# Two of three matrix products of a feed-forward block regrouped after Strassen, on one NeuronCore

## The reference

```python
def swiglu(x, w_gate, w_up, w_down):
    return (jax.nn.silu(x @ w_gate) * (x @ w_up)) @ w_down
...
h = h + 0.5 * swiglu(rms_norm(h, ffn1_norm[l]), ffn1_w_gate[l], ffn1_w_up[l], ffn1_w_down[l])
...
h = h + 0.5 * swiglu(rms_norm(h, ffn2_norm[l]), ffn2_w_gate[l], ffn2_w_up[l], ffn2_w_down[l])
```

## Time and profile before

| | us |
|---|---|
| median of 3 runs | 1800.49 (1800.37 to 1800.58) |
| the profiled execution: first to last instruction | 1798.8 |
| PE busy | 1790.1 (100%) |
| DVE busy | 1072.4 (60%) |
| ACT busy | 775.2 (43%) |
| POOL busy | 206.1 (11%) |

### The profile page before, as it was taken

How to read it: one execution, slowest core, us unless ns; L and a number is a source line. 1 busy time by engine, 2 the same in 40 slices (tenths; PEclk the granted TensorE clock), 3 DMA queues, 4 the chain that set the end, 5 groups by cost and what they waited for, 6 DMA issues and landing times.

```text
span 1798.8 us, 22927 instructions
## 1 busy us (share of the span) xinstructions
PE 1790.1 (100%) x8322; PEld 1472.2 (82%) x8322; DVE 1072.4 (60%) x1339; ACT 775.2 (43%) x1103; POOL 206.1 (11%) x174
## 2 busy tenths in 40 slices
PE   9999999999999999999999999999999999999998
PEld 7888888888777788888888888888888888888887
DVE  6444443342778665444443348877577586868985
ACT  5333332223555544333333335454353454466673
POOL 3000000011000002000001110110201102213333
PEclk9999999999999999999999999999999999999999
DMA  4332333344321232332233323232222222233233
GB/s 157 99 99 93 94 105 105 105 145 131 110 77 60 70 95 94 97 101 93 93 99 106 107 93 105 89 99 94 83 94 87 93 85 80 85 106 106 94 129 117
DMA packets 51506, 178.63 MB, mean 99 GB/s; under 512 B 6168, under 2 KB 8344, under 8 KB 51440
## 3 DMA queue, kind: packets, MB, share of 16 engines
q1 hardware_dynamic: 48624, 169.10, 29.4%
q0 software_dynamic: 2384, 8.21, 1.5%
q10 hardware_dynamic: 432, 0.40, 0.1%
HBM read 173.48 MB, written 2.11 MB: 98 GB/s over the span
## 4 chain that ended last, share of the span: by engine, by line
PE 98%; DVE 1%; ACT 0%; DMA 0%; issue 0%; POOL 0%; ACTq 0%; DVEq 0%
PE banks L548 29%; PE banks L550 29%; PE banks L549 29%; PE banks L711 1%; PE banks L730 1%; PE banks L754 1%; PE banks L889 1%; PE banks L891 1%; PE banks L890 1%; PE banks L917 0%; PE banks L915 0%; PE banks L916 0%; PE banks L674 0%; PE banks L675 0%; PE banks L676 0%; PE banks L1101 0%
## 5 line engine op out<-in xcount | busy, mean ns | idle before, releaser
L1784 DVE TENSOR_TENSOR w_lo<-w_raw,w_hi 128x1024 fp32r<-128x1024 f32 x313 | 397.5, 1270 | 528.5 <-ACT w_hi L1187 527.6
L548 PE MATMUL banks<-u_hi,w_hi 128*128 128x512 f32 x1528 | 599.5, 392 | 0.8 <-DVE u_lo L1801 0.8
L550 PE MATMUL banks<-u_hi,w_lo 128*128 128x512 f32 x1528 | 595.0, 389 | 0.0
L549 PE MATMUL banks<-u_lo,w_hi 128*128 128x512 f32 x1528 | 594.6, 389 | 0.0
L1187 ACT ACTIVATE w_hi<-w_raw 128x1024 fp32r<-128x1024 f32 x313 | 331.4, 1059 | 512.5 <-PE banks L550 475.1
L548 PEld LDWEIGHTS banks<-u_hi,w_hi 128*128 128x128 f32 x1528 | 286.9, 188 | 61.6 <-issue 2.4
L550 PEld LDWEIGHTS banks<-u_hi,w_lo 128*128 128x128 f32 x1528 | 286.8, 188 | 60.5
L549 PEld LDWEIGHTS banks<-u_lo,w_hi 128*128 128x128 f32 x1528 | 287.0, 188 | 58.9 <-issue 0.5
L548 PE MATMUL banks<-hid_hi,w_hi 128*128 128x512 f32 x352 | 136.9, 389 | 0.0
L549 PE MATMUL banks<-hid_lo,w_hi 128*128 128x512 f32 x352 | 136.9, 389 | 0.0
L550 PE MATMUL banks<-hid_hi,w_lo 128*128 128x512 f32 x352 | 136.9, 389 | 0.0
(11 more groups left out here) (342 smaller groups left out, 2425.9 us busy)
## 6 DMA issues: line engine op xcount, KB each, us to landing
w_raw<-weights SPq DMA_DIRECT2D x315, 512.0 KB, 3.5
bias<-neighbour_bias POOLq DMA_DIRECT2D x8, 384.0 KB, 5.1
v_win<-v_a POOLq DMA_DIRECT2D x16, 128.0 KB, 5.0
out_t<-x SPq DMA_DIRECT2D x16, 128.0 KB, 1.8
x<-x_t SPq DMA_DIRECT2D x3, 512.0 KB, 6.7
nm<-gate_rows POOLq DMA_DIRECT2D x4, 256.0 KB, 4.1
fl<-gate_rows POOLq DMA_DIRECT2D x4, 256.0 KB, 3.6
rope<-rope_table POOLq DMA_DIRECT2D x1, 512.0 KB, 5.5
```

The lines of the kernel that those rows point to most:

```text
L548: nc.tensor.matmul(o, wh, hi, start=start and k == 0, stop=False)
L549: nc.tensor.matmul(o, wh, lo, start=False, stop=False)
L550: ins = nc.tensor.matmul(o, wl, hi, start=False, stop=stop and k == len(pairs) - 1)
L1784: nc.vector.tensor_tensor(w_lo[:, n.slot, :], w_raw[:, n.slot, :], w_hi[:, n.slot, :].bitcast(F32), ALU.subtract)\
```

## The change

Of the 22 chunks of gate and up, 6 stay as they were. The other 16 are taken in 8 pairs of two chunks. For a pair the weights are a 2 x 2 arrangement (up and gate; first and second half of the width), the values too (halves of the width; halves of the tokens). Their 8 partial products become 7, after Strassen's scheme in Winograd's form, with 256 tokens each. Product k of pair p is (k, p) in the list `SP_SEQ` (56 products, 24 matmuls with 256 columns each).

- **Values.** DVE writes the normalised values in full (`full`, to `uf`, 8 instructions beside the last plain chunks), makes four sums of quarters (`combo_sum`), and both engines split these and three plain quarters (`combo_high`, `quarter_high` on ACT; `combo_low`, `quarter_low` on DVE: 7 of each).
- **Weights.** POOL loads five matrices of 512 KB a pair (`load_matrices`): `m1` (two buffers), `m2`, `m3`, `m4` and `mx` (one buffer each). DVE makes four sums in place (`first_sums` two, `later_sum`, `last_sum`). Each of the seven is split by `mat_high` (ACT) and `mat_low` (DVE) into one of four buffers (`slot_of`), so product j reuses that of product j-4.
- **Results.** Products 1, 6, 7, 4 add up in one bank; ACT copies its state after 1, 6 and 7 (`snap_p1`, `snap_p6`, `snap_p7`) and takes silu of it after 4 (`silu_first`), and the next of them waits for the copy. DVE adds products 2, 5 and 3 to the copies (`up_first`, `gate_second`, `up_second`), then `silu_second` (ACT), `hid_first`, `hid_second` (DVE), `pair_high` (ACT), `pair_low` (DVE).
- **Down.** The 22 blocks of a column are summed in three parts, of chunks 0 to 5, 6 to 13 and 14 to 21. Each part has 8 columns, one unit each, each added to `x` by itself. The first stands after the plain chunks, the second after product (1, 5), the third after the last product.

TensorE's waits in `pair_product`, beside `m_lo` for the weights: product 1 waits for `silu_first` two pairs earlier; 6, 7 and 4 for the copy after 1, 6 and 7; 3 for `gate_second`; 2 and 5 for the sums two pairs earlier. `snap_p1` to `snap_p7` wait for their product.

```diff
+F_PLAIN = 6
+N_SP = 8
+DOWN_PARTS = (range(0, F_PLAIN), range(F_PLAIN, 14), range(14, F_CHUNKS))
+U_FFN = 2 * F_PLAIN + 3 * DC
...
+def sp_products():
+    seq = [(5, 0), (1, 0), (6, 0), (2, 0), (7, 0)]
+    for p in range(N_SP - 1):
+        seq += [(1, p + 1), (4, p), (5, p + 1), (6, p + 1), (3, p), (7, p + 1), (2, p + 1)]
+    return seq + [(4, N_SP - 1), (3, N_SP - 1)]
+SP_SEQ = sp_products()
+N_PROD = len(SP_SEQ)
+SP_AT = {kp: j for j, kp in enumerate(SP_SEQ)}
+SP_SLOT = [(j + 2) % 4 for j in range(N_PROD - 1)] + [2]
+SP_SLOT_FREE = [max([i for i in range(j) if SP_SLOT[i] == SP_SLOT[j]], default=None) for j in range(N_PROD)]
+SP_LAST_IN = [max(j for j in range(N_PROD) if SP_SLOT[j] == k) for k in range(2)]
+DOWN1_AFTER = SP_AT[1, 5]
+DOWN1_SLOT_FREE = [max(j for j in range(DOWN1_AFTER + 1) if SP_SLOT[j] == k) for k in range(2)]
+SP_BANKS = ((3, 4), (5, 6), (7, 2))
+H1, H2 = slice(0, T // 2), slice(T // 2, T)
...
+        def slot_of(pair, pair2, j):
+            k = SP_SLOT[j]
+            return pair[:, k, :] if k < 2 else pair2[:, k - 2, :]
+        def product_source(k, p):
+            return (None, m1[:, p % 2, :], m2[:, :], m2[:, :], m4[:, :], mx[:, :], m1[:, p % 2, :], m3[:, :])[k]
...
+            def pair_product(f, j):
+                k, p = SP_SEQ[j]
+                q = N_SP * f + p
+                o = bank[SP_BANKS[{2: 1, 5: 2, 3: 2}.get(k, 0)][p % 2]]
+                pe.wait_ge(m_lo, N_PROD * f + j + 1)
+                if j == 0:
...
+                wh, wl = slot_of(w_hi, w_hi2, j), slot_of(w_lo, w_lo2, j)
+                fresh = k in (1, 2, 5)
+                for c in range(2):
+                    for kk in range(4):
+                        if k <= 3:
+                            kh, half = QUARTERS[k - 1]
+                            hi, lo = u_hi[:, 4 * kh + kk, half], u_lo[:, 4 * kh + kk, half]
+                        else:
+                            t = (T4, T1, T2, T3)[k - 4]
+                            hi, lo = xs_hi[:, t, kk * 256:(kk + 1) * 256], xs_lo[:, t, kk * 256:(kk + 1) * 256]
+                        b = slice((2 * kk + c) * P, (2 * kk + c + 1) * P)
+                        half_bank = o[:, c * 256:(c + 1) * 256]
+                        nc.tensor.matmul(half_bank, wh[:, b], hi, start=fresh and c == 0 and kk == 0, stop=False, skip_group_check=True)
+                        nc.tensor.matmul(half_bank, wh[:, b], lo, start=False, stop=False, skip_group_check=True)
+                        ins = nc.tensor.matmul(half_bank, wl[:, b], hi, start=False, stop=kk == 3, skip_group_check=True)
+                ins.then_inc(m_used, 1)
...
+            def down_columns(f, part, u0, g0):
+                chunks = DOWN_PARTS[part]
+                for m in range(DC):
+                    n, g = Lin(u0 + 2 * F_PLAIN + DC * part + m), Lin(g0 + 2 * F_PLAIN + DC * part + m)
+                    unit_ready(n)
+                    bank_free(g)
+                    for k in range(len(chunks)):
+                        if m == 0 and part == 0:
+                            pe.wait_ge(hid_lo_ready, (F_PLAIN + N_SP) * f + k + 1)
+                        if m == 0 and part > 0 and k % 2 == 0:
+                            pe.wait_ge(hid_lo_ready, pairs_split(f, 4 * (part - 1) + k // 2))
+                        product(bank[g.slot][:, :], [(k, hid_hi[:, k, :], hid_lo[:, k, :])], n, k == len(chunks) - 1,
+                                start=k == 0, stop=k == len(chunks) - 1)
...
+                down_columns(f, 0, u0, g0)
+                for j in range(DOWN1_AFTER + 1):
+                    pair_product(f, j)
+                down_columns(f, 1, u0, g0)
+                for j in range(DOWN1_AFTER + 1, N_PROD):
+                    pair_product(f, j)
+                down_columns(f, 2, u0, g0)
...
+                def mat_high(j):
+                    k, p = SP_SEQ[j]
+                    q = N_SP * f + p
+                    if k == 1:
+                        act.wait_ge(m1_loaded[p % 2], 16 * (q // 2 + 1))
+                    if k == 2:
+                        act.wait_ge(m2_loaded, 16 * (q + 1))
...
+                    if SP_SLOT_FREE[j] is not None:
+                        act.wait_ge(m_used, N_PROD * f + SP_SLOT_FREE[j] + 1)
+                    if j in (2, 3):
+                        act.wait_ge(unit_used, down[0] + DC - 3 + j)
+                    if j in (DOWN1_AFTER + 1, DOWN1_AFTER + 2):
+                        act.wait_ge(unit_used, down[1] + DC - 2 + j - DOWN1_AFTER)
+                    nc.scalar.activation(slot_of(w_hi, w_hi2, j), product_source(k, p), ACT.Copy).then_inc(m_hi, 1)
...
+                for m in range(DC - 2):
+                    split_raw(Lin(down[0] + 2 + m))
+                    if m < 4:
+                        combo_high((T1, T3, T2, T4)[m], m + 1)
+                    else:
+                        quarter_high(m - 4)
+                quarter_high(2)
+                for j in range(4):
+                    mat_high(j)
+                snap_p1(0)
+                mat_high(4)
+                for p in range(N_SP - 1):
+                    at = SP_AT[1, p + 1]
+                    snap_p6(p)
+                    mat_high(at)
+                    if at == DOWN1_AFTER:
+                        act.wait_ge(m_used, N_PROD * f + DOWN1_SLOT_FREE[0] + 1)
+                        split_raw(Lin(down[1]))
+                        snap_p7(p)
+                        pair_high(p - 1)
+                        act.wait_ge(m_used, N_PROD * f + DOWN1_SLOT_FREE[1] + 1)
+                        split_raw(Lin(down[1] + 1))
+                        snap_p1(p + 1)
+                        silu_second(p)
+                        for m in range(DC - 2):
+                            split_raw(Lin(down[1] + 2 + m))
+                    mat_high(at + 1)
+                    if at != DOWN1_AFTER:
+                        snap_p7(p)
+                        if p >= 1:
+                            pair_high(p - 1)
+                    mat_high(at + 2)
+                    mat_high(at + 3)
+                    if at != DOWN1_AFTER:
+                        snap_p1(p + 1)
+                        silu_second(p)
+                    mat_high(at + 4)
+                    silu_first(p)
+                    mat_high(at + 5)
+                    mat_high(at + 6)
...
+                for i in range(F_PLAIN - 2, F_PLAIN):
+                    for m in range(4):
+                        full(4 * (i - F_PLAIN + 2) + m)
+                    chunk(i, Lin(u0 + 2 * i), Lin(g0 + 2 * i))
+                pairs_low(f, u0, g0)
...
+                def first_sums(p):
+                    q = N_SP * f + p
+                    dve.wait_ge(m1_loaded[p % 2], 16 * (q // 2 + 1))
+                    dve.wait_ge(m3_loaded, 16 * (q + 1))
+                    dve.wait_ge(mx_ready, 16 * (q + 1))
+                    nc.vector.tensor_tensor(mx[:, :], mx[:, :], m3[:, :], ALU.add).then_inc(m_summed, 1)
+                    nc.vector.tensor_tensor(m3[:, :], m1[:, p % 2, :], m3[:, :], ALU.subtract).then_inc(m_summed, 1)
...
+                    dve.wait_ge(m_summed, 4 * q + 1)
+                    dve.wait_ge(m_lo, N_PROD * f + SP_AT[1, p] + 1)
+                    nc.vector.tensor_tensor(m1[:, p % 2, :], mx[:, :], m1[:, p % 2, :], ALU.subtract).then_inc(m_summed, 1)
+                def last_sum(p):
+                    q = N_SP * f + p
+                    dve.wait_ge(m_summed, 4 * q + 3)
+                    dve.wait_ge(m_lo, N_PROD * f + SP_AT[2, p] + 1)
+                    nc.vector.tensor_tensor(m2[:, :], m2[:, :], m1[:, p % 2, :], ALU.subtract).then_inc(m_summed, 1)
...
+                for m in range(DC):
+                    if m < DC - 2:
+                        split_lo(Lin(down[0] + 2 + m))
+                    if m < 4:
+                        combo_sum((T1, T3, T2, T4)[m])
+                    else:
+                        combo_low((T1, T3, T2, T4)[m - 4], m - 3)
+                    if m >= 5:
+                        quarter_low(m - 5)
+                    down_add(0, m)
+                first_sums(0)
+                mat_low(0)
+                mat_low(1)
+                later_sum(0)
+                mat_low(2)
+                mat_low(3)
+                last_sum(0)
+                mat_low(4)
+                for p in range(N_SP - 1):
+                    at = SP_AT[1, p + 1]
+                    mat_low(at)
+                    if p >= 1:
+                        up_second(p - 1)
+                        hid_second(p - 1)
+                    if at == DOWN1_AFTER:
+                        split_lo(Lin(down[1]))
+                        pair_low(p - 1)
+                        split_lo(Lin(down[1] + 1))
+                        up_first(p)
+                        gate_second(p)
+                        first_sums(p + 1)
+                        later_sum(p + 1)
+                        for m in range(DC):
+                            if m < DC - 2:
```

(69 more changed lines are left out.)

273 lines of the change are left out of this document (244 added, 29 removed).

## The result

| | before | after |
|---|---|---|
| median, us | 1800.53 (1800.37 to 1800.81) | 1826.62 (1823.0 to 1827.8) |
| the profiled execution, first to last instruction | 1798.8 | 1825.4 |

What follows compares the result with a forecast made beforehand. TensorE, busy 1790 of 1798.8 us, was taken as the bound. A block's 12.8 us saved against its waits gave +4.55 us, two +9.1, on the median 1800.5: 1809.6 us; range 1795 to 1830.

Steps and rivals of the forecast that it cites:

- step 1: TensorE's products in the pairs: seven 256-column products replace four units, saving 1.60 us a pair, 12.8 us a block.
- step 2: From the plain chunks into down part 0: the first column's last block waits 2.1 us for `hid_lo` of chunk 5.
- step 3: Inside down part 0: sums and splits delay the reading of banks, columns come 4.5 us apart, 3.1 us lost.
- step 4: From part 0 into the pairs: TensorE idle 5.2 us ahead of (5, 0), then 0.95 us at (6, 0).
- step 5: Steady pairs: a ring through the load of `m2`, 21.1 us against 20.16 of products, loses 3.6 us a block.
- step 6: Around parts 1 and 2: waits of 2.2 and 0.2 us, 2.4 us a block; POOL's queue nothing, or 1 us.
- rival (d): The clock falls in the idle 5.2 us before the pairs; slow products cost 2.6 to 5.1 us a block; chance 0.15.
- Rival (a): Part 0 and its end, 10.4 us of waits: junctions are cheap and the change is faster, 1797.3 or 1794.3; chance 0.14.
- Its last sentence: On the price of matmuls: at 109 ns the 56 products would save 14.5 us a block more, mostly returned by the ring.
- step 1's own 18.9 us: Saving a block in the products by the Trainium skill's formula, 109 and 216 ns a matmul; the forecast used the rows instead.
- Step 5's upper end: Ring loss in the steady pairs if the load takes 5.5 us: 12.3 us a block.
- Nothing, or 1 us: Cost forecast for POOL's queue, whose loads stand between `norm_sum` calls and share the engines with SP's stream.

Runs made afterwards that it cites:

- a_order: The changed kernel with only the order of instructions on DVE and ACT altered in part 0 and at part 1, no arithmetic removed: 1800.73 us, ratio 0.9999.
- a_m2_two: The changed kernel with a second buffer for `m2`: 1816.38 us, ratio 1.0083.
- filler: The changed kernel with 20 matmuls of ones on ones between part 0 and product (5, 0), 8 between part 1 and (4, 4): 1816.65 us, ratio 1.0088.
- b_loads_small: The kernel before with 80 added POOL loads of one 4 KB row each into a tile nobody reads: 1806.89 us, ratio 1.0035.
- b_loads_big: The kernel before with 80 added POOL loads of 512 KB each into a tile nobody reads: 1807.16 us, ratio 1.0033.
- a_sp: The changed kernel with the matrices loaded from SP's queue instead of POOL's: 1812.98 us, ratio 1.0068.

## Why the prediction was right or wrong

| us, one block | forecast | block 1 | block 2 |
|---|---|---|---|
| step 1, the products | -12.8 | -12.8 | -12.8 |
| step 2, `hid_lo` of chunk 5 | 2.1 | 2.2 | 2.2 |
| step 3, inside part 0 | 3.1 | 3.1 | 3.1 |
| step 4, idle ahead of (5, 0) | 5.2 | 5.0 | 5.0 |
| step 4, (6, 0) | 0.95 | 1.0 | 1.0 |
| step 5, the ring | 3.6 | 5.6 | 5.5 |
| step 6, part 1 and the end | 2.4 | 2.2 | 2.2 |
| the clock behind waits | rival (d) | 3.1 | 4.2 |
| the rest | none | 0.15 | 0.05 |
| sum | 4.55 | 9.5 | 10.4 |

All are read from start to start, as the forecast counts them: a wait and the slower first matmul behind it, 0.1 us at 512 columns and 0.07 at 256. The slow products behind the idle stretches are in the row of the clock.

**Right: steps 1, 2, 3, 4, and 6 inside the block.** A product takes 2.88 us and its matmuls start 0.120 us apart, at 1344 matmuls a block. The junctions could be worked out from durations and the written order to within 0.25 us. Step 3 had column 7 start 27.55 us after the end of column 0. It started 27.54 us after it (27.56 in block 2):

```profile
80.75 0.39 PE L635 MATMUL banks<-hid_hi,w_hi 128*128 128x512 f32 x1
...
108.29 0.47 PE L635 MATMUL banks<-hid_hi,w_hi 128*128 128x512 f32 x1 [1.00 <-DVE x L2081]
```

The columns before it came 4.43 to 4.46 us apart, where 4.5 were reckoned. Rival (a), cheap junctions, falls for the change as it was written; `a_order` shows that it is true of the work itself. Its last sentence mixes two prices: 14.5 us takes 109 ns for the new matmuls and 227 ns for the old ones; by step 1's own 18.9 us, which prices both alike, it would be 6.1 us. Step 5's upper end, 12.3 us with a load of 5.5, comes to about 12.0 by its own terms.

**Wrong by size, step 5.** The term is the load in the ring. It was put at 3.8 us "since here nothing else is queued then". The five loads of `m2` ahead of the gaps took 4.2 us in the mean of each block: 3.6 to 4.25 us, and once in each block more, 5.04 and 5.71. That is 0.4 us above the forecast for each of five gaps, 2 us a block. `mx` and `m3` are issued right behind all of them but the last, which has nothing behind it and took 3.58 and 3.67 us, the shortest. That fits loads that share the DMA engines, but with filler 19 of 24 took 3.6 to 3.85 us with the same two behind them, and no run took the two away: the cause of the longer landings is not shown. The gap from `mat_low` to POOL's issue was 0.29 us and not SP's 0.17. The pairs where the ring binds came 21.4 and 21.6 us apart at (7, 3) and (7, 4) of block 1, and not 21.1. The mechanism, its place (ahead of product (7, p); none ahead of (7, 5), where part 1 stands) and its cure (`a_m2_two`) were right; the loss was 5.6 and 5.5 us instead of 3.6 a block, 3.9 us in all.

**Wrong, step 6: "Nothing, or 1 us" for POOL's queue.** I counted what POOL's loads delay while the work goes on, and not what they add to the end of the program: 6.3 us. The row was there to be read in the trace of before, a drain of 4605 ns at the end, but it did not show what it depends on; the two kernels with extra loads do.

**Wrong, the forecast's exclusion of rival (d).** The row on which it rests, a clock of 0.53 where TensorE had stopped, was the right one. "It was dense work before here, so it may hold" was the guess that failed: the clock fell in each block behind the idle 5 us, and TensorE had been busy for 10.89 of the 12 us before it. After work without a gap it fell too: behind part 1, 43.60 us of it, a wait of 2.08 us was enough, in three of the four blocks of the changed kernel's two traces. Waits of that length (d) did not count at all. In the forecast's sum the products behind a wait are priced at 2.88 us, so this term stands at nothing. It gave 2.6 to 5.1 us a block; 3.1 and 4.2 were measured. Its chance of 0.15 was too low.

The difference between forecast and result adds up: 6.3 for the drain, 7.3 for the clock, 3.9 for the ring, 0.3 for step 2 and (6, 0), 0.2 for the rest of the blocks and 0.3 outside of them, less 0.8 for steps 3, 4 and 6, are the 17.5 us (26.6 - 9.1).

## What to carry to other kernels

When TensorE is the bound and an algorithm saves a fraction of its work, ask of each extra sum on the other engines whether it stands in the queue ahead of something that TensorE waits for next. Here their place alone was worth 25.9 us, and the saving itself 25.6. Price a wait of TensorE above its own length, since matmuls behind it may run at half clock, and keep the array busy where the wait can't be removed. Look at a buffer whose reload is released late in the cycle, with all that is issued right behind that load, and count DMAs issued by POOL once more for the end of the program.

## What the runs showed of the hardware

- POOL's drain at the end of the program takes 4.6 us with 38 DMAs issued by POOL and 11.13 us with 118, 0.082 us for each of the 80 more on average, whether they move 4 KB or 512 KB each (`b_loads_small`, `b_loads_big`). With the same loads issued by SP it is 4.6 us (`a_sp`).
- The granted clock fell to 0.50 behind a wait of 5.0 us in 8 of 8 blocks, in block 1 of the changed kernel with TensorE busy for 10.89 of the 12 us before it. Behind one of 2.08 us after 43.60 us without a gap it fell in 6 of 8, behind one of 2.05 us in the first column of part 0 in 6 of 16. At that level matmuls of 256 columns start 0.21 us apart instead of 0.120, and a product of 2.88 us takes 4.4 to 5.3.
- Matmuls of ones on ones held the clock at 1.00 through the waits ahead of (5, 0) and (4, 4) in all four blocks of two traces, and the first product behind them then took 2.97 us.
